# A two-block transformer on one core: the context norm placed inside the second feed-forward stage, its key products placed among the norms that follow

## The chip, the cores and the metric

The kernel runs on one core of one Trainium2 chip. The metric is the device time of one execution in microseconds (us), and the median of the runs shown is compared. Everything is float32.

## The reference, cut to what matters

A first block (256 tokens, width 1024) ends in a feed-forward layer, `y = conv_ffn(rms_norm(x))`, `x = x + rms_norm(y)`. The second block then takes `x` and a separate context of 256 tokens. Both are normed and modulated with their own shift and scale, and both go through the same input projections:

```
u  = modulate(rmsnorm(x,   norm1_g), sh1,  sc1)
uc = modulate(rmsnorm(ctx, norm1_g), sh1c, sc1c)
pl = split_proj(u,  w_in)      # queries, keys, values, gates, ...
pc = split_proj(uc, w_in)      # of the context, keys, values and gates alone are used
```

After that come a chunked recurrence (mLSTM) and a differential attention over context and latent keys, their merge, and a mixture of 32 experts (384 slabs of weights of 1 MB). The context and its norm depend on nothing in the first block. `x` depends on all of it.

## The kernel before

The activations lie transposed: 128 features in the partitions, 8 tiles of 256 tokens. The weights come in slabs of 1 MB. SP loads them in the order of a table, `SCHEDULE` (L59), into a ring of five slots, and waits before each load until the slab five places earlier has been used (`slab_used`, L388). TensorE multiplies in units: one unit (`product`) is 16 matmuls of 128x256, of which the trace records two each, so 32 records. The units go round three PSUM banks, and a unit waits until the unit three before it has been read.

The order on each engine is written out by hand, and the engines meet by semaphores. Around the change it is this:

- **Second feed-forward, in** (`ffn_in(1)`, TensorE L746): 22 units, one slab each. Per unit VectorE scales the bank (L1388) and adds two taps of a convolution (L1399), ScalarE makes the first tap (L1090) and a Silu (L1096), and VectorE multiplies (L1408). Unit 0 comes with the norm n7, whose squares VectorE adds up first (`presum`, L1380), so that one matmul (`presummed`, L623) gives the mean.
- **Second feed-forward, out** (`ffn_out(1, "n8")`, L638 and L649), with the squares of its result (L1078) and the mean for the norm n8 (`stat`, L607) at its end.
- **The norms n8, nc and n9.** A norm is a chain over three engines: squares on ScalarE (L1051), the mean by 8 matmuls with a constant matrix (`stat`, L607), a square root on ScalarE (`root`, L1059), a reciprocal on VectorE (`rstd`, L1352), and the scaled tiles. n8 norms the feed-forward's result and adds it to `X` (`residual`, L1368 and L1371). nc is the context's: SP loads it into `CT` (L477) once the feed-forward has ended, and VectorE and ScalarE write its modulated form `UC` (L1547, L1188). n9 norms `X`, and its modulated form is `H` (the same lines).
- **The first projections of the second block**: `mq` (2 slabs, 2 units, from `H` alone), the gates (64 matmul records of 16 columns, L767), `mk` (2 slabs, 4 units: each slab times `UC` and times `H`), then `cumf` (L777), `mv` and the rest.

TensorE's order there reads:

```
ffn_out(1, "n8")
stat("nc", 1, mean)
pe.wait_ge(sem("nc_root"), before("nc_root") + 1)
stat("n9", 0, mean)
stage("mq", H, "n9_h", busy=7)     # 7 matmuls without use ahead of the wait
...                                # gates
two("mk")
pe.wait_ge(sem("logf"), 1)         # then cumf
```

The last 40% of the time are the experts, whose slabs go round 16 slots (`first_load` L464, then L529).

Of the kernel before, what the change touches and what calls it, by code (L numbers as in the profile page):

```python
# [20 lines left out]
T = 256  # L21
D = 1024
KT = D // P
D_FF = 2816
FT = D_FF // P
TAPS = 31
GROUPS = 3
HEADS = 8
# [7 lines left out]
ADA_SLABS = 24  # L36
# [150 lines left out]
def build(nc, d_x, d_ctx, d_par, d_con, d_mmask, d_rows, d_gatew, d_routerw, d_b1, d_b2, d_cond, d_dense, d_experts, d_out):  # L187
    ctx = ExitStack()
    with ctx:
# [4 lines left out]
        norms = ["n0", "ln", "n1", "n2", "n3", "n4", "n6", "n7", "n8", "nc", "n9"]  # L194
        shared = {}
        for kind, count, stages in (
                ("sq", KT, norms + ["hm", "do", "n10", "n11"]), ("sum", 1, norms + ["n10", "n11"]),
                ("root", 1, norms + ["n10", "n11"]), ("x", KT, ["n1", "n3", "n6", "n8"]),
                ("h", KT, ["n0", "n2", "n4", "n5", "n7", "n11"]), ("h", KT, ["ln", "nc", "n9", "n10"]),
                ("p", KT, ["nc", "n9", "n10"]), ("tap", 2 * FT, ["ffn0", "ffn1"]), ("silu", FT, ["ffn0", "ffn1"]),  # L200
                ("act", FT, ["ffn0", "ffn1"]), ("cv", 2 * FT, ["ffn0", "ffn1"]), ("presum", KT - 1, ["n2", "n4", "n7"]),
                ("acc", KT, ["ffn0", "ffn1"]), ("out_slab", FT // 2, ["ffn0", "ffn1"])):
            for i, s in enumerate(stages):
                shared[f"{s}_{kind}"] = (f"{kind}_from_{stages[0]}_on", i * count)
# [71 lines left out]
        UC = tiles(area(NB, 2048), KT)  # L276
# [3 lines left out]
        HM = tiles(area(NB + 9216, 2048), KT)  # L280
# [144 lines left out]
        for i in range(2):  # L425
            second.append((FIRST_UNIT["mq"] + i, [MQ[:, 2 * i + j, :] for j in range(2)]))
        for name, to in (("mk", MK), ("mv", MV), ("dq", DQ), ("dk", DK), ("dv", DV)):
            for i in range(SLABS_OF[name]):
                if name == "dq":
                    second.append((FIRST_UNIT[name] + i, [to[:, 2 * i + j, :] for j in range(2)]))  # L430
                    continue
                for half in range(2):
                    if name in ("mk", "dk"):
# [23 lines left out]
        def _(sp):  # L457
# [8 lines left out]
            for g in range(DENSE_SLABS):  # L466
# [72 lines left out]
        def _(pe):  # L539
# [80 lines left out]
            def presummed(name):  # L620

                pe.wait_ge(sem(name + "_presum"), before(name + "_presum") + KT - 1)
                nc.tensor.matmul(banks[STAT][:, T:2 * T], mean, SQ[:, 0, :], start=True, stop=True)\  # L623
                    .then_inc(sem(name + "_sum"), 1)
# [145 lines left out]
            two("mk")  # L770
# [274 lines left out]
        def _(act):  # L1045
            def square(name, src, ready=None, sq=SQ):

                for c in range(KT):
# [31 lines left out]
            def ffn_in(layer):  # L1080
                name = f"ffn{layer}_in"
                for j in range(FT + 1):
                    if j < FT:
# [96 lines left out]
            ffn_in(1)  # L1180
            squared_acc(1, "n8")
            root("n8", 0)

            def shifted(name, v, m, dst):

                for c in range(KT):
# [22 lines left out]
            take(0, 2)  # L1209
# [5 lines left out]
            take(2, len(second))  # L1215
# [128 lines left out]
        def _(dve):  # L1344
# [29 lines left out]
            def presum(name):  # L1374

                for c in range(1, KT):
# [5 lines left out]
            def ffn_in(layer):  # L1382
                name = f"ffn{layer}_in"
                for j in range(FT + 1):
                    if j < FT:
# [145 lines left out]
            ffn_in(1)  # L1531

            dve.wait_ge(sem("ada_done"), ada_products(ADA_SLABS))
            for v in range(2):
                me(V.tensor_tensor(MOD[:, 0:16, v], MOD[:, 0:16, v], par[:, PAR["ada_b"]:PAR["ada_b"] + 16], ALU.add))
                me(V.scalar_tensor_tensor(GS1[:, :, v], MOD[:, 8:16, v], 1.0, par[:, PAR["norm1"]:PAR["norm1"] + 8],
                                          ALU.add, ALU.mult))
            dve.wait_ge(sem("rows_in"), 16)
            lam = rows[:, 0:256].rearrange("p (a b d) -> p a b d", a=2, b=2)
            me(V.tensor_tensor(tiles(LW, 2), lam[:, :, 0, :], lam[:, :, 1, :], ALU.mult))  # L1540
            V.tensor_reduce(LAM[:, 0:2], tiles(LW, 2), AX.X, ALU.add).then_inc(sem("lam_dot"), 1)
            residual("n8", rstd("n8", 0), acc, lambda c: ("ffn_post", 8 + c))

            def modulated(name, r, src, gain, dst):

                for c in range(KT):
# [11 lines left out]
            modulated("nc", rstd("nc", 1), CT, lambda c: GS1[:, c, 1:2], UC)  # L1558
# [4 lines left out]
            take(0, 2)  # L1563
# [15 lines left out]
            take(2, 6)  # L1579
# [347 lines left out]
```

## Time and profile before

| | |
|---|---|
| time, median of 3 runs | 2514.79 us (2513.84 to 2515.28) |
| time of the profiled execution | 2513.32 us |
| its span, first to last instruction | 2511.2 us |
| mean granted clock of TensorE | 0.989 of full speed |
| TensorE busy | 2391.6 us (95%) |
| VectorE busy | 760.0 us (30%) |
| ScalarE busy | 412.0 us (16%) |
| moved by DMA | 606.98 MB, mean 242 GB/s |

The span is 2.1 us shorter than the time of the same execution. The busy shares are averages over stages with different limits. So the stretches around the change are read one by one: which engine waits there, for what, and how long each step takes.

### The profile page before, as it was taken

The page shows a single profiled execution, that of the slowest core. Times are in us where ns is not written, and L with a number is a line of the kernel's source. Part 1 is how long each engine was busy: PE and PEld are TensorE (multiplying, and loading weights), DVE is VectorE, ACT ScalarE, POOL GpSimd, SP SyncE. Part 2 cuts the span into 40 slices and gives each one's busy share as a digit, 9 for nine tenths or more (in the row PEclk, how much of TensorE's full clock was granted, in tenths as well). Part 3 has the DMA queues.
Part 4 walks back from the last instruction along what each step waited for, and adds up shares of the span by engine and source line. Part 5 has one row for each costly group of instructions (what it writes and reads, how often), then busy time and mean ns, then how long its engine had stood idle before and what let it go on. Part 6 is the DMA issues. An engine that isn't in the chain of part 4 may idle for free.

```text
span 2511.2 us, 32943 instructions
## 1 busy us (share of the span) xinstructions
PE 2391.6 (95%) x13498; PEld 1800.1 (72%) x13498; DVE 760.0 (30%) x1846; ACT 412.0 (16%) x941; POOL 0.2 (0%) x4
## 2 busy tenths in 40 slices
PE   8899999999899999999988898999999999999998
PEld 7688888888788887988866586555555555555554
DVE  5833374210434312000244642222212111111212
ACT  4232202010232203000023422110101010101101
POOL 0000000000000000000000000000000000000000
PEclk9999999999999999899999999999999999999999
DMA  6034475664224442132122173999999999999996
GB/s 254 34 118 151 151 285 218 219 235 172 78 80 147 156 155 110 58 117 84 67 84 84 51 289 128 395 421 421 421 422 421 422 421 422 421 421 421 422 422 271
DMA packets 84281, 606.98 MB, mean 242 GB/s; under 512 B 9376, under 2 KB 9760, under 8 KB 10560
## 3 DMA queue, kind: packets, MB, share of 16 engines
q1 hardware_dynamic: 84192, 605.73, 61.1%
q8 instruction: 63, 1.03, 0.2%
q14 instruction: 26, 0.21, 0.0%
HBM read 604.65 MB, written 1.05 MB: 241 GB/s over the span
## 4 chain that ended last, share of the span: by engine, by line
PE 72%; SPq 15%; DVE 6%; ACT 3%; issue 2%; DMA 2%; DVEq 0%; ACTq 0%
PE bank L567 27%; SPq L529 15%; PE bank L980 10%; PE bank L564 8%; PE bank L638 5%; PE bank L1007 5%; PE bank L556 3%; DVE arena L1478 2%; PE bank L581 2%; PE bank L943 2%; PE bank L974 2%; PE bank L607 1%; DMA arena<-in_experts 1%; PE bank L718 1%; PE bank L649 1%
## 5 line engine op out<-in xcount | busy, mean ns | idle before, releaser
L567 PE MATMUL bank<-arena,ring 128*128 128x256 f32 x3296 | 716.3, 380 | 0.0
L567 PEld LDWEIGHTS bank<-arena,ring 128*128 128x128 f32 x3296 | 629.0, 191 | 83.9
L980 PE MATMUL bank<-arena 128*64 128x256 f32 x2048 | 293.7, 383 | 6.8 <-DMA arena<-in_experts 4.4
L980 PEld LDWEIGHTS bank<-arena 128*64 128x64 f32 x2048 | 173.7, 137 | 96.8 <-issue 20.0
L1839 DVE TENSOR_SCALAR arena<-bank 128x256 f32<-128x256 f32 x64 | 27.2, 425 | 698.2 <-PE bank L980 698.2
L564 PE MATMUL bank<-ring,arena 128*128 128x256 f32 x896 | 196.3, 382 | 0.0
L564 PEld LDWEIGHTS bank<-ring,arena 128*128 128x128 f32 x896 | 171.8, 192 | 23.2
L980 PE MATMUL bank<-ring,arena 128*64 128x256 f32 x1280 | 176.3, 382 | 8.0 <-DMA ring<-in_experts 5.1
L980 PEld LDWEIGHTS bank<-ring,arena 128*64 128x64 f32 x1280 | 104.6, 137 | 75.7 <-issue 13.9
L1007 PE MATMUL bank<-arena 128*64 128x512 f32 x512 | 140.1, 594 | 3.0 <-ACT arena L1326 3.0
L638 PE MATMUL bank<-arena,ring 128*128 128x256 f32 x576 | 124.6, 380 | 0.0
L638 PEld LDWEIGHTS bank<-arena,ring 128*128 128x128 f32 x576 | 109.7, 190 | 14.6
L980 PE MATMUL bank<-spare,arena 128*64 128x256 f32 x768 | 117.5, 383 | 0.2
L1311 ACT ACTIVATE arena<-arena 128x256 f32<-128x256 f32 x64 | 26.7, 417 | 456.3 <-DVE arena L1839 456.2
L1007 PEld LDWEIGHTS bank<-arena 128*64 128x64 f32 x512 | 49.8, 137 | 66.3 <-issue 66.3
L1456 DVE SCALAR_TENSOR_TENSOR arena<-ring,arena 128x1024 f32<-128x1024 f32 x64 | 74.9, 1220 | 73.6 <-DMA ring<-in_dense 73.6
L1399 DVE SCALAR_TENSOR_TENSOR arena<-arena,par 128x254 f32<-128x254 f32 (+1 forms) x176 | 73.3, 479 | 51.0 <-ACT arena L1090 51.0
L581 PE MATMUL bank<-arena,ring 128*128 128x256 f32 x384 | 87.0, 384 | 0.0
L1090 ACT ACTIVATE arena<-arena,par 128x256 f32<-128x256 f32 x88 | 48.0, 592 | 229.8 <-DVE arena L1388 229.8
L980 PEld LDWEIGHTS bank<-spare,arena 128*64 128x64 f32 x768 | 69.2, 137 | 22.7 <-issue 5.0
L581 PEld LDWEIGHTS bank<-arena,ring 128*128 128x128 f32 x384 | 72.2, 191 | 18.1 <-issue 9.1
L974 PE MATMUL bank<-arena 32*64 32x256 f32 x512 | 83.1, 400 | 0.9 <-ACT arena L1306 0.9
(263 smaller groups left out, 2159.2 us busy)
## 6 DMA issues: line engine op xcount, KB each, us to landing
arena<-in_experts SPq DMA_DIRECT2D x192, 1024.0 KB, 25.9
ring<-in_dense SPq DMA_DIRECT2D x186, 1024.0 KB, 4.8
ring<-in_experts SPq DMA_DIRECT2D x120, 1024.0 KB, 26.5
spare<-in_experts SPq DMA_DIRECT2D x72, 1024.0 KB, 25.9
con<-in_con SPq DMA_DIRECT2D x1, 1248.0 KB, 12.3
X<-in_x SPq DMA_DIRECT2D x1, 1024.0 KB, 5.0
arena<-in_cond SPq DMA_DIRECT2D x1, 1024.0 KB, 17.7
arena<-in_ctx SPq DMA_DIRECT2D x1, 1024.0 KB, 4.7
```

The costliest lines, as they stand in the source:

```text
L529: sp.dma_start(expert_slab(j), src).then_inc(slot_sem(j), 16)
L556: ins = nc.tensor.matmul(half_of(u, j), w[:, k, j * P:(j + 1) * P], src[:, k, :], start=(k == 0 and j == 0), stop=(k == KT - 1), skip_grou ...
L564: ins = nc.tensor.matmul(o, src[:, k, j * P:(j + 1) * P], w[:, k, :], start=(k == 0), stop=(k == KT - 1))
L567: ins = nc.tensor.matmul(o, w[:, k, j * P:(j + 1) * P], src[:, k, :], start=(k == 0), stop=(k == KT - 1))
L581: ins = nc.tensor.matmul(o, w[:, k, j * P:(j + 1) * P], H[:, k, :], start=(k == 0), stop=(k == KT - 1))
L638: ins = nc.tensor.matmul(banks[WORK + m // 2][:, (m % 2) * T:(m % 2 + 1) * T], w[:, kk, m * P:(m + 1) * P], F_ACT[:, k, :], start=(k == 0 ...
L943: ins = nc.tensor.matmul(banks[4 + b][:, (c % 4) * P:(c % 4 + 1) * P], U2T[:, t, c * P:(c + 1) * P], SEL[:, t, :], start=(t == 0), stop=(t ...
L974: nc.tensor.matmul(o, ONEH[:, e * CAP:(e + 1) * CAP], B1[:, i * T:(i + 1) * T], start=True, stop=False)
L980: ins = nc.tensor.matmul(o, XGT[:, k, e * CAP:(e + 1) * CAP], w[:, k, :], start=False, stop=(k == KT - 1))
L1007: ins = nc.tensor.matmul(banks[2 + half][e * CAP:(e + 1) * CAP, :], ACTT[:, k, e * CAP:(e + 1) * CAP], w[:, kk, half * 512:(half + 1) * 51 ...
L1399: ins = V.scalar_tensor_tensor(o, F_U[j % 2][:, half, 0:T - back], par_col("ffn_dw", (layer * 3 + 2 - back) * 44 + c), o, ALU.mult, ALU.add)
L1456: V.scalar_tensor_tensor(JUNK[:, n % 3, :], w[:, j, :], 1.0, CSR[:, v, :], ALU.mult, ALU.mult, accum_out=MOD[:, 2 * i + j, v:v + 1]).then_ ...
```

## The change

1. The context is loaded right before slab 1 of `ffn1_in`, after the attention's last head has been written (`att_out`), and no more behind the whole feed-forward.
2. The norm nc runs inside `ffn_in(1)`, by a function that ScalarE and VectorE call at the head of each unit j: the squares at j = 3 to 6, their sum on VectorE at j = 5 to 8, one matmul with the sum after unit 10 on TensorE, the root at j = 12, the reciprocal at j = 14, scaling at 15 to 18 and shift at 16 to 19, two tiles each. The work that makes the modulation (six small VectorE instructions) moves from the feed-forward's end to j = 2.
3. In `SCHEDULE`, `mk` stands ahead of `mq`. TensorE's order after the feed-forward is: unit mk0 x `UC`, the mean for n9, mk1 x `UC`, mk0 x `H`, mk1 x `H`, the gates, then both `mq` units. A slab of `mk` is given back when its `H` unit has ended. The seven matmuls without use are gone.
4. `UC` lies where `HM` lies later, as the old place is in use by the feed-forward.

```diff
-    ("mq", 2, 2), ("mk", 2, 4), ("mv", 4, 8),
+    ("mk", 2, 4), ("mq", 2, 2), ("mv", 4, 8),
...
-        UC = tiles(area(NB, 2048), KT)
...
-        HM = tiles(area(NB + 9216, 2048), KT)
+        UC = HM = tiles(area(NB + 9216, 2048), KT)
...
+            elif name == "mk":
+                unit_ready(eng, FIRST_UNIT[name] + 2 + i)
...
-                if g == SLAB_AT["mq", 1]:
-
-                    sp.wait_ge(sem("ffn1_out_slab"), before("ffn1_out_slab") + 11)
+                if g == SLAB_AT["ffn1_in", 1]:
+
+                    sp.wait_ge(sem("att_out"), HEADS)
                     sp.dma_start(CT, d_ctx).then_inc(sem("ctx_in"), 16)
...
-            stage("ffn1_in", H, first=1, count=21)
+            stage("ffn1_in", H, first=1, count=10)
+            presummed("nc", 0)
+            stage("ffn1_in", H, first=11, count=11)
             ffn_out(1, "n8")
-            stat("nc", 1, mean)
-            pe.wait_ge(sem("nc_root"), before("nc_root") + 1)
-            stat("n9", 0, mean)
...
-            stage("mq", H, "n9_h", busy=7)
-
             pe.wait_ge(sem("nc_h"), before("nc_h") + KT)
+            product(FIRST_UNIT["mk"], SLAB_AT["mk", 0], UC)
+            stat("n9", 0, mean)
+            product(FIRST_UNIT["mk"] + 1, SLAB_AT["mk", 1], UC)
+            product(FIRST_UNIT["mk"] + 2, SLAB_AT["mk", 0], H,
+                    wait_chunk=lambda k: pe.wait_ge(sem("n9_h"), before("n9_h") + k + 1))
+            product(FIRST_UNIT["mk"] + 3, SLAB_AT["mk", 1], H)
...
-            two("mk")
+            stage("mq", H)
...
+            def context_norm(j):
+
+                if j == 3:
+                    act.wait_ge(sem("ctx_in"), 16)
+                    act.wait_ge(sem("n7_sum"), before("n7_sum") + 1)
+                if 3 <= j < 7:
+                    square("nc", lambda c: CT[:, c, :], first=2 * j - 6, end=2 * j - 4)
+                if j == 12:
+                    root("nc", 0)
+                if 16 <= j < 20:
+                    shifted("nc", 1, 0, UC, first=2 * j - 32, end=2 * j - 30)
...
+            ffn_in(1, context_norm)
+            squared_acc(1, "n8")
+            root("n8", 0)
...
-            act.wait_ge(sem("ctx_in"), 16)
-            square("nc", lambda c: CT[:, c, :])
-            root("nc", 1)
             square("n9", lambda c: X[:, c, :], "n8_x")
             root("n9", 0)
-            shifted("nc", 1, 0, UC)
             shifted("n9", 0, 0, H)
...
-            take(0, 2)
+            take(0, 4)
...
+            def context_norm(j):
+
+                if j == 2:
+                    first_shift()
+                if 5 <= j < 9:
+                    presum("nc", max(2 * j - 10, 1), 2 * j - 8)
+                if j == 14:
+                    rstd("nc", 0)
+                if 15 <= j < 19:
+                    modulated("nc", RS[:, 0:T], CT, lambda c: GS1[:, c, 1:2], UC, first=2 * j - 30, end=2 * j - 28)
...
+            ffn_in(1, context_norm)
+            residual("n8", rstd("n8", 0), acc, lambda c: ("ffn_post", 8 + c))
...
-            modulated("nc", rstd("nc", 1), CT, lambda c: GS1[:, c, 1:2], UC)
             modulated("n9", rstd("n9", 0), X, lambda c: GS1[:, c, 0:1], H)
```

**TensorE, from the end of the second feed-forward to the first instruction of cumf.** Before, without what only repeats (L649 is the feed-forward's last product; L607 the means of n8, nc and n9, in this order 4, 8 and 8 of the 20; L543 the matmuls without use; L556 and L567 units; L767 the gates; L777 cumf):

```order
L649 MATMUL bank<-arena,ring 128x256 x8
L607 MATMUL bank<-arena,con 128x256 [waits sq_from_n0_on] x12
L607 MATMUL bank<-arena,con 128x256 [waits sq_from_n0_on,root_from_n0_on]
L607 MATMUL bank<-arena,con 128x256 [waits sq_from_n0_on] x7
L543 MATMUL bank<-con 128x256 [waits read0,slab2]
L556 MATMUL bank<-arena,ring 128x256 [waits h_from_ln_on]
L567 MATMUL bank<-arena,ring 128x256 [waits read1,slab3]
L767 MATMUL bank<-small,arena 128x16 [waits gatew_in,x_from_n1_on,h_from_ln_on]
L567 MATMUL bank<-arena,ring 128x256 [waits read2,slab4,h_from_ln_on]
L777 MATMUL bank<-arena,con 128x4 [waits logf]
```

Of the change (its lines stand 2 to 5 lower: L651, L609, L569, L558, L772, L782):

```order
L651 MATMUL bank<-arena,ring 128x256 x8
L609 MATMUL bank<-arena,con 128x256 [waits sq_from_n0_on] x4
L569 MATMUL bank<-arena,ring 128x256 [waits read0,slab2,h_from_ln_on]
L609 MATMUL bank<-arena,con 128x256 [waits sq_from_n0_on] x8
L569 MATMUL bank<-arena,ring 128x256 [waits read1,slab3]
L558 MATMUL bank<-arena,ring 128x256 [waits h_from_ln_on,read2,slab2]
L569 MATMUL bank<-arena,ring 128x256 [waits read0,slab3]
L772 MATMUL bank<-small,arena 128x16 [waits gatew_in,x_from_n1_on]
L569 MATMUL bank<-arena,ring 128x256 [waits read1,slab4]
L782 MATMUL bank<-arena,con 128x4 [waits logf]
```

The eight matmuls of nc's mean are gone from here, n9's eight stand between two units with `UC`, and between the gates and cumf there are two units where there were four.

**ScalarE, inside the second `ffn_in`, at j = 12.** Of the change (L1097 is the first tap, L1103 the Silu, L1062 and L1064 the root):

```order
L1097 ACTIVATE arena<-arena,par 128x256 x2
L1103 ACTIVATE arena<-arena 128x256
L1062 ACT_TABLE_LOAD
L1062 ACTIVATE small<-small 128x1
L1064 ACTIVATE arena<-bank,small 128x256
L1097 ACTIVATE arena<-arena,par 128x256 x2
L1103 ACT_TABLE_LOAD
L1103 ACTIVATE arena<-arena 128x256
```

Before, the pair of L1090 and L1096 (now L1097 and L1103) repeats there with nothing between; the root's three instructions and two loads of a function table are new in this place.

## Rows read from the trace of the kernel before

**Rows 1.** The page, part 4: the chain that ended last, by engine.
```profile
PE 72%; SPq 15%; DVE 6%; ACT 3%; issue 2%; DMA 2%; DVEq 0%; ACTq 0%
```

**Rows 2.** Windows, expert stage: busy of PE, PEld, DVE, ACT, POOL, PEclk, DMA share, GB/s.
```profile
1520.00:1560.00 40.00, 32.41 (x154) 25.85 (x153) 15.80 (x66) 13.18 (x27) 0.00 (x0) 0.87 0.28 105
...
1700.00:1800.00 100.00, 98.60 (x722) 55.76 (x720) 18.70 (x60) 11.01 (x21) 0.00 (x0) 1.00 1.01 421
```

**Rows 3.** Waits of SP's queue: us in total, times, longest us.
```profile
SPq L464 <- PE bank L980: 71.8, 12, 30.3
```

**Rows 4.** Timeline of PE, the mean of n8: start us, us, line, operation.
```profile
973.70 1.89 PE L607 MATMUL bank<-arena,con 128*128 128x256 f32 x8
```

**Rows 5.** The chain in order of time, n8 to cumf: start us, us, what.
```profile
973.89 4.74 DMA arena<-in_ctx
...
979.13 6.48 PE bank L607 x16
...
986.55 3.71 PE bank L607 x16
...
994.39 7.17 PE bank L556 x32
...
1008.47 10.12 PE bank L767 x64
1018.59 29.60 PE bank L567 x128
```

**Rows 6.** Groups by line from 751 to 897 us: busy us, mean ns, idle.
```profile
L567 PE MATMUL bank<-arena,ring 128*128 128x256 f32 x672 | 145.2, 380 | 0.0
```

**Rows 7.** Timeline of DVE, end of n8 and the norm n9.
```profile
983.41 0.75 DVE L1371 TENSOR_TENSOR X<-X,arena 128x256 f32<-128x256 f32 x2
...
991.10 1.75 DVE L1352 RECIPROCAL arena<-arena 128x256 f32<-128x256 f32 x1
992.88 3.26 DVE L1547 SCALAR_TENSOR_TENSOR arena<-X,small,arena 128x256 f32<-128x256 f32 x8
```

**Rows 8.** Timeline of ACT, the norm n9 (and nc's eight shifts ahead of its own).
```profile
986.00 2.55 ACT L1051 ACTIVATE arena<-X 128x256 f32<-128x256 f32 x8
...
990.28 0.47 ACT L1059 ACTIVATE arena<-bank,small 128x256 f32<-128x256 f32 x1 [1.64 <-PE bank L607]
990.66 6.47 ACT L1188 ACTIVATE arena<-arena,small 128x256 f32<-128x256 f32 x16
```

**Rows 9.** Windows around the norms and the gates, columns as in rows 2.
```profile
979.00:986.00 7.00, 6.47 (x16) 4.93 (x16) 5.16 (x15) 2.68 (x10) 0.00 (x0) 0.59 1.02 428
...
1008.00:1013.00 5.00, 5.00 (x42) 4.95 (x40) 0.76 (x2) 0.00 (x0) 0.00 (x0) 0.90 0.63 210
1013.00:1018.00 5.00, 5.00 (x25) 5.00 (x25) 0.00 (x0) 0.00 (x0) 0.00 (x0) 0.50 0.00 0
```

**Rows 10.** Timeline of DVE, last step of the chain that gives logf.
```profile
1021.20 0.39 DVE L1576 SCALAR_TENSOR_TENSOR arena<-arena 128x16 f32<-128x16 f32 x2 [1.93 <-ACT arena L1214]
```

**Rows 11.** Timeline of DVE: a presum, and first and last instruction now at j = 2.
```profile
746.78 3.59 DVE L1380 TENSOR_TENSOR arena<-arena 128x256 f32<-128x256 f32 x7
...
900.61 0.17 DVE L1535 TENSOR_TENSOR small<-small,par 128x16 f32<-128x16 f32 x1
...
901.75 0.29 DVE L1541 TENSOR_REDUCE small<-small 128x2 f32<-128x128 f32 x1
```

**Rows 12.** Timeline of DVE, start of a unit of the second ffn_in.
```profile
771.95 0.69 DVE L1388 TENSOR_TENSOR arena<-bank,arena 128x512 f32<-128x512 f32 x1 [3.05 <-PE bank L567]
```

**Rows 13.** Timeline of ACT, a table load and a unit of the same stage.
```profile
759.97 1.28 ACT L1096 ACT_TABLE_LOAD   x1
...
772.68 1.09 ACT L1090 ACTIVATE arena<-arena,par 128x256 f32<-128x256 f32 x2 [5.51 <-DVE arena L1388]
```

**Rows 14.** Timeline of SP: after the attention, and in the feed-forward's second half.
```profile
713.48 44.91 SPq L501 DMA_DIRECT2D ring<-in_dense  x6
...
930.73 14.14 SPq L501 DMA_DIRECT2D ring<-in_dense  x3
```

More of the change, by code:

```diff
@@ L190, in build @@
         sems = {}
[L194 removed]
+        norms = ["n0", "ln", "n1", "n2", "n3", "n4", "n6", "n7", "nc", "n8", "n9"]
         shared = {}
@@ L424, in build @@
         second = []
-        for i in range(2):
-            second.append((FIRST_UNIT["mq"] + i, [MQ[:, 2 * i + j, :] for j in range(2)]))
-        for name, to in (("mk", MK), ("mv", MV), ("dq", DQ), ("dk", DK), ("dv", DV)):
+        for half in range(2):
+            for i in range(2):
+                second.append((FIRST_UNIT["mk"] + 2 * half + i, [MK[:, 2 * i + j, half * T:(half + 1) * T] for j in range(2)]))
+        for name, to in (("mq", MQ), ("mv", MV), ("dq", DQ), ("dk", DK), ("dv", DV)):
             for i in range(SLABS_OF[name]):
-                if name == "dq":
+                if name in ("mq", "dq"):
                     second.append((FIRST_UNIT[name] + i, [to[:, 2 * i + j, :] for j in range(2)]))
@@ L618, in out_stage, with presummed @@
                 stat(stat_name, 0, mean, first=6)
-            def presummed(name):
+            def presummed(name, half=1):
                 pe.wait_ge(sem(name + "_presum"), before(name + "_presum") + KT - 1)
-                nc.tensor.matmul(banks[STAT][:, T:2 * T], mean, SQ[:, 0, :], start=True, stop=True)\
+                nc.tensor.matmul(banks[STAT][:, half * T:(half + 1) * T], mean, SQ[:, 0, :], start=True, stop=True)\
                     .then_inc(sem(name + "_sum"), 1)
@@ L1045, in _, with square @@
         def _(act):
-            def square(name, src, ready=None, sq=SQ):
-                for c in range(KT):
+            def square(name, src, ready=None, sq=SQ, first=0, end=KT):
+                for c in range(first, end):
                     if ready:
@@ L1078, in squared_acc, with ffn_in @@
                         nc.scalar.activation(SQ[:, i, :], acc(i), ACT.Square).then_inc(sem(name + "_sq"), 1)
-            def ffn_in(layer):
+            def ffn_in(layer, beside=None):
                 name = f"ffn{layer}_in"
                 for j in range(FT + 1):
+                    if beside:
+                        beside(j)
                     if j < FT:
@@ L1179, in _, with shifted @@
             root("n7", 1)
[L1180 to L1186, printed above, removed]
+            def context_norm(j):
[8 more added lines that the diff above has]
+                    shifted("nc", 1, 0, UC, first=2 * j - 32, end=2 * j - 30)
+            def shifted(name, v, m, dst, first=0, end=KT):
+                for c in range(first, end):
                     act.wait_ge(sem(name + "_p"), before(name + "_p") + c + 1)
@@ L1214, in _ @@
             nc.scalar.activation(AB, AB, ACT.Ln, bias=ONE_COL).then_inc(sem("f_ln"), 1)
-            take(2, len(second))
+            take(4, len(second))
             def raw_gate(n):
@@ L1372, in residual, with presum @@
                          .then_inc(sem(name + "_x"), 1)
-            def presum(name):
-                for c in range(1, KT):
+            def presum(name, first=1, end=KT):
+                for c in range(first, end):
                     dve.wait_ge(sem(name + "_sq"), before(name + "_sq") + c + 1)
@@ L1380, in presum, with ffn_in @@
                     V.tensor_tensor(SQ[:, 0, :], SQ[:, 0, :], SQ[:, c, :], ALU.add).then_inc(sem(name + "_presum"), 1)
-            def ffn_in(layer):
+            def ffn_in(layer, beside=None):
                 name = f"ffn{layer}_in"
                 for j in range(FT + 1):
+                    if beside:
+                        beside(j)
                     if j < FT:
@@ L1530, in _ @@
             rstd("n7", 1)
[L1531 to L1546, printed above, removed]
+            def first_shift():
+                dve.wait_ge(sem("ada_done"), ada_products(ADA_SLABS))
+                for v in range(2):
+                    me(V.tensor_tensor(MOD[:, 0:16, v], MOD[:, 0:16, v], par[:, PAR["ada_b"]:PAR["ada_b"] + 16], ALU.add))
+                    me(V.scalar_tensor_tensor(GS1[:, :, v], MOD[:, 8:16, v], 1.0, par[:, PAR["norm1"]:PAR["norm1"] + 8],
+                                              ALU.add, ALU.mult))
+                dve.wait_ge(sem("rows_in"), 16)
+                lam = rows[:, 0:256].rearrange("p (a b d) -> p a b d", a=2, b=2)
+                me(V.tensor_tensor(tiles(LW, 2), lam[:, :, 0, :], lam[:, :, 1, :], ALU.mult))
+                V.tensor_reduce(LAM[:, 0:2], tiles(LW, 2), AX.X, ALU.add).then_inc(sem("lam_dot"), 1)
@@ new lines, in context_norm, with modulated @@
+            def context_norm(j):
[7 more added lines that the diff above has]
+                    modulated("nc", RS[:, 0:T], CT, lambda c: GS1[:, c, 1:2], UC, first=2 * j - 30, end=2 * j - 28)
+            def modulated(name, r, src, gain, dst, first=0, end=KT):
+                for c in range(first, end):
@@ L1562, in _ @@
             me(V.tensor_scalar(LAM[:, 5:6], LAM[:, 4:5], -1.0, -LAM_INIT, ALU.mult, ALU.add))
-            take(0, 2)
+            take(0, 4)
             dve.wait_ge(sem("gates"), 1)
@@ L1578, in _ @@
                 me(ins) if d == 0 else ins.then_inc(sem("logf"), 1)
-            take(2, 6)
+            take(4, 6)
             dve.wait_ge(sem("cumf"), 1)
```

4 lines of the change are left out of this document (2 added, 2 removed).

## The prediction

> **What bounds the kernel now.** First the chain that ended last, by engine [rows 1]: 72% of it is TensorE, 15% SP's queue. The queue's part lies in the last 500 us, where the experts' slabs come at 421 GB/s with a DMA share of 1.01 [rows 2]. So the question is whether time won early reaches the end. Between 1520 and 1560 us the DMA share is 0.28, and the queue's first loads of experts wait for TensorE, 71.8 us in 12 waits [rows 3]. The stream starts when TensorE lets it, so a start earlier by x us ends it earlier by x.
>
> Then the stretch itself, from the chain in order of time. The eight records of n8's mean end at 973.70 + 1.89 = 975.6 us [rows 4]. TensorE waits for the context, whose load of 4.74 us was issued only at 973.89 [rows 5]. It does the 16 records of nc's mean (6.48 us) and the 16 of n9's (3.71 us), waits again, and starts `mq` at 994.39 [rows 5]. The first unit whose result is used begins 18.8 us after 975.6. Then come 14.08 us of `mq`, 10.12 us of gates and 29.60 us of `mk`, up to 1048.19 [rows 5]. The stretch is **72.6 us** from 975.6 to cumf.
>
> **The change, part by part.** A unit is 32 records. The 672 records of the feed-forward, 21 units, took 145.2 us without a pause [rows 6], so a unit is 6.91 us and 16 records are 3.45 us.
>
> *TensorE after the feed-forward.* The two units with `UC` need nothing of the first block, and `UC` is ready long before.
> - mk0 x `UC`: 975.6 to 982.5 us.
> - The mean for n9, 3.45 us: to 986.0. Can it run without a pause? The last tile of `X` is written at 983.41 + 0.75 = 984.16 [rows 7], and its square takes 0.4 us (8 squares in 2.55, overlapping) [rows 8], so it is there at 984.6. The matmul that needs it starts at 985.5. No pause.
> - mk1 x `UC`: to 992.9. Beside it the chain of n9 runs: root 0.47 [rows 8], reciprocal 1.75, first scaled tile 0.5 [rows 7], first shift 0.5 (16 in 6.47) [rows 8]. The first tile of `H` is there at 986.0 + 3.3 = 989.3, the last at 992.1 (8 scalings in 3.26 and one shift). TensorE wants the first at 992.9. No pause, with 3.6 us to spare.
> - mk0 x `H` and mk1 x `H`: 13.8 us, to 1006.7.
> - The gates 10.12 us, as before, to 1016.8.
> - The two `mq` units: 13.8 us at the full clock, and a surcharge. Before, the 128 records behind the gates took 29.60 us where four units are 27.65, so 1.95 us were lost at their start. I take the same 1.95. To 1032.6.
>
> *In `ffn_in`* TensorE gets one more matmul, two records, 0.43 us.
>
> The sum is 6.91 + 3.45 + 6.91 + 13.82 + 10.12 + 13.82 + 1.95 + 0.43 = **57.4 us**, against 72.6: **15.2 us less**. Removed are 3.5 us of waiting for the context, nc's mean (6.48) and most of the wait for n9, and two units of 6.91 fill what is left.
>
> *What bounds the surcharge and the gates.* The granted clock was 0.90 from 1008 to 1013 us and 0.50 from 1013 to 1018, that is, it fell from 2.4 to 1.2 GHz while TensorE did gates of 16 columns; 42 records went in the first window and 25 in the second [rows 9]. If it did not fall, 64 gate records would take 64 x 5/42 = 7.6 us and nothing would be lost behind them: 2.5 + 1.95 = 4.5 us less than my sum. If it fell at their start, 64 x 5/25 = 12.8 us, 2.7 more, and a stretch like that of 979 to 986, where 16 records took 6.47 us at 0.59 [rows 9] instead of 3.45, would add 3.0. I take the value in between, the one measured on the same 64 matmuls. What precedes the gates differs: before, TensorE paused twice in the 33 us ahead of them, now it doesn't, so a fall would come later rather than earlier. The Trainium skill ("TensorE: Matmul & The Clock Gate", Part 1) says that the clock is either half or full, never between, and that the number of slow matmuls differs from run to run of one and the same kernel. By it neither end of this bound can be excluded, and the sum would be 57.4 with some 5 us to either side. The trace agrees as far as it goes: 0.50 in one window, 1.00 in most.
>
> *The cover of the gate arithmetic.* cumf waits for logf, which was ready at 1021.20 + 0.39 = 1021.6, 3.0 us after the gates' end at 1018.6 [rows 5, 10]. It was covered by 29.6 us of `mk`, now by 15.8 us of `mq`. Nothing to pay. If it were late, cumf would be next.
>
> *The work put inside `ffn_in`.* VectorE gets six small instructions at j = 2 (900.61 to 902.04, 1.4 us), a presum (3.6 us) [rows 11], a reciprocal (1.75) and eight scalings (3.3) [rows 7]: 10.0 us. It waits 3.05 us of each 6.91 us unit for TensorE [rows 12]. The largest piece at one j is 1.75. ScalarE gets eight squares (2.6), eight shifts (3.2), and at j = 12 a root (0.47) with two table loads of 1.28 [rows 13], 3.0 us: 8.8 us in all. It waits 5.51 us of each unit [rows 13]. Both fit unit by unit; at j = 12 the later Silu holds up VectorE's product by about 3.0 us, which just uses up its 3.05 idle. TensorE wants a bank back only two further units later, 13.8 us. The cost is nothing. Without that cover it would be 18.8 us (rival D). Nor do the stage's last units carry anything new.
>
> *Loads.* Slab 1 of `ffn1_in` was issued at 713.48 [rows 14], behind o's first unit. The context now goes ahead of it, once the attention's last head is out, and takes 4.74 us. The slab is wanted at about 751, where the row of the 672 records begins [rows 6], so some 30 us are free. `mk` stands where `mq` stood: the three loads from 930.73 to 944.87 [rows 14] end with the first slab after the feed-forward's, so mk0 is issued by 945, 30 us before its use, and mk1 some 7 us later. The two slabs of `mk` are held until 999.8 and 1006.7; the loads behind them are mv1 and mv2, wanted after 1050. Nothing.
>
> **The number.** The profiled execution took 2513.32 us, 2.1 above its span. Less 15.2 that is 2498.1. The median shown is 1.5 us above that execution, so for the median I predict 2514.79 - 15.2 = **2499.6 us**.
>
> **Rivals.** A measurement of this kernel can tell about 0.2%, 5 us, from no change.
> - **A, the forecast**: chance 0.84, 2495 to 2505 with the clock's two bounds (+5.7, -4.5).
> - **B, n9 comes late.** TensorE works in order, and n9's mean now stands behind a unit: it ends at 986.0, 1.4 us after the last square. If the chain to the first tile of `H` took over 6.9 us instead of 3.3, TensorE would wait at mk0 x `H`, and the clock could fall as at 979 us: 2 us of waiting and 3.0 of slowness make 2504.6. For it: TensorE's 7 matmuls without use are gone, so a wait would be idle. Against: 3.6 us of room. Chance 0.06.
> - **C, nothing reaches the end.** If the experts' stream, 421 GB/s for 900 us, were already held by DMA when it starts, the time would stay 2514.8. For it: SP's 15% of the chain. Against: the share of 0.28 at its start [rows 2] and the waits of the first loads [rows 3]. Chance 0.05.
> - **D, slower: the three banks run dry in `ffn_in`.** If VectorE's lag adds up beyond the 13.8 us of two units, TensorE stands still inside the feed-forward, in front of each further piece. It decides from about 3 us of added work per unit on, kept up for several units. In full series the added work is 18.8 us, and a clock that falls at its three stops (squares, root, shifts, 3.0 each as at 979) makes it 27.8: 27.8 - 15.2 = 12.6 us slower, 2527.4. For it: the two table loads and three engines in turn for one norm. Against: each piece is smaller than the idle time of its unit. Chance 0.05. The Trainium skill ("ScalarE: Activation LUTs", What ACT_TABLE_LOAD costs, and its advice to do all of one table set before switching) puts each switch at about 2.66 us with a drain. By it j = 12 would hold 2 x 2.66 + 0.47 = 5.8 us in 5.51 of idle, 0.3 us over, once. The trace shows 1.28 us and the next instruction right behind.
>
> **How the numbers follow.** The likeliest case gives 2499.6. The range 2495.0 to 2505.0 holds A with both ends of the clock and B. C and D lie outside, 0.10 together, and some of A's ends. Faster by over 5 us: A and B, 0.90. Within 5 us: C, 0.05. Slower: D, 0.05.
>
> **What would show it.** In the changed profile the records of mk0 x `UC` begin within 0.1 us of the end of n8's mean, and TensorE has no idle time until cumf; that stretch is about 57 us. `ffn_in`'s units keep 6.91 us each with one break of 0.43. SP issues the context at about 707 us, one unit before 713.48. The first expert load comes 15 us earlier, and DMA runs at 421 GB/s as long as before. I am wrong if TensorE waits at mk0 x `H` (B), if the start of the stream moves and the end doesn't (C), or if the 22 units of `ffn_in` take over 153 us (D). A different clock around the gates would show as a size error alone.

## The result, and the profile after

| | before | after |
|---|---|---|
| median of the runs timed together | 2514.32 us (2512.52 to 2515.28, 4 runs) | **2540.03 us** (2538.78 to 2541.35, 4 runs) |
| ratio after to before | | **1.0096**, 95% interval 1.0084 to 1.0108 |
| profiled execution, its span | 2513.32 us, 2511.2 us | 2540.68 us, 2538.8 us |

The changed kernel is 25.7 us slower. The prediction was 15.2 us faster, with 0.05 for slower. It was wrong, and not by a size: the sign is the other one.

The part of the program that was changed did what was forecast. This is the chain that ended last in the changed kernel, in order of time from n8's mean to cumf (start us, us, what):

```profile
975.48 1.73 PE bank L609 x8
977.21 6.91 PE bank L569 x32
984.11 3.45 PE bank L609 x16
987.57 6.91 PE bank L569 x32
994.47 6.91 PE bank L558 x32
1001.38 6.91 PE bank L569 x32
1008.29 8.43 PE bank L772 x64
1016.72 15.85 PE bank L569 x64
1032.57 4.36 PE bank L782 x40
```

Each row starts where the row above ends. From n8's end at 977.21 to cumf at 1032.57 are 55.4 us, where it was 72.6 [rows 4, 5]. cumf starts 15.6 us earlier than the 1048.19 of before, as n8's mean itself ends 1.6 us later here. That lead lasts: the first matmul of the loop over the pairs of experts starts at 1544.59 instead of 1560.09 us, 15.5 earlier.

The loss lies behind that point. Three places of the page show it; its header, the queue that brings TensorE's instructions (packets, MB, share of 16 engines) and the chain by engine, after:

```profile
span 2538.8 us, 32902 instructions
...
q8 instruction: 126, 2.06, 0.3%
...
PE 87%; DVE 7%; ACT 3%; issue 3%; DMA 0%; ACTq 0%; DVEq 0%
```

and the same of before:

```profile
span 2511.2 us, 32943 instructions
...
q8 instruction: 63, 1.03, 0.2%
```

SP's queue had 15% of the chain [rows 1] and has none now; TensorE has 87%. The bound has changed. And the queue that brings instructions moved twice as many packets of 16 KB in an execution of 41 instructions fewer.

The chain in the expert loop, after (start us, us, what), tells when. L1012 is the down projection that ends a pair, L979 and L985 are the first matmuls of the next:

```profile
1645.22 13.95 PE bank L1012 x64
1659.17 2.26 issue
1661.43 0.75 PE bank L979 x4
1662.18 2.26 PE bank L985 x9
1664.44 2.33 issue
1666.77 5.38 PE bank L985 x23
...
1711.39 13.95 PE bank L1012 x64
1725.34 0.58 PE bank L979 x4
...
1768.59 13.95 PE bank L1012 x64
1782.54 2.02 issue
```

The loop's body holds two pairs. Within it, at 1725.34, the next pair follows at once. Where TensorE jumps back, at 1659.17 and at 1782.54, it stands still twice, 2.26 us and, after 13 matmuls, 2.33 us, and waits for nothing that the profile shows. The matmuls between and behind the pauses are slow. The windows there (columns as in rows 2) give the clock:

```profile
1659.17:1672.15 12.98, 8.39 (x39) 5.11 (x39) 0.00 (x0) 1.07 (x2) 0.00 (x0) 0.62 1.01 418
1700.00:1800.00 100.00, 94.19 (x648) 53.30 (x642) 16.00 (x53) 8.90 (x18) 0.00 (x0) 0.95 1.00 411
```

The granted clock fell, to 0.62 over these 13 us; in a stretch without a jump it is 1.00 [rows 2]. The waits of TensorE (line, us in total, times, longest) say how often, after:

```profile
PE bank L985 <- issue: 17.8, 7, 3.6
PE bank L979 <- issue: 14.7, 7, 2.3
```

There are 7 of each, one for each jump back. One repetition takes 1768.59 - 1645.22 = 123.4 us; before it took 1775.13 - 1660.72 = 114.4 us (the starts of the same L1007 rows in its chain). That is 9.0 us more, 4.6 of it pauses and 4.4 slow matmuls; seven times that would be 63 us.

The whole loop, from its first matmul record to the end of its last, took 932.4 us before (1560.09 to 2492.44) and takes 975.9 now (1544.59 to 2520.50): 43.5 us more. Less the lead of 15.5 these are 28.0 us, and the two spans differ by 27.6. The jumps cost more than the 43.5, because before the change TensorE waited in the loop for the experts' stream: its wait list has these rows (line, us in total, times, longest), and the changed kernel's has none of them.

```profile
PE bank L980 <- DMA arena<-in_experts: 7.3, 10, 0.7
PE bank L980 <- DMA ring<-in_experts: 5.1, 7, 0.7
PE bank L980 <- DMA spare<-in_experts: 2.2, 3, 0.7
```

Together these are 14.6 us. TensorE is now the later of the two. Runs below, without the stream, put the price of the seven jumps at **60.4 us** and that former wait at 16.9.

### The profile page after: what moved, and what is told of

It reads as the page before. It is cut to its first block, busy times and chain, and to the rows that moved or that the text cites. A ratio compares the mean times of both kernels' runs of the same rounds, so it can differ in the third digit from the quotient of the medians.

```text
span 2538.8 us, 32902 instructions
## 1 busy us (share of the span) xinstructions
PE 2407.8 (95%) x13470; PEld 1807.1 (71%) x13470; DVE 762.2 (30%) x1853; ACT 415.4 (16%) x943; POOL 0.2 (0%) x4
## 3 DMA queue, kind: packets, MB, share of 16 engines
HBM read 604.65 MB, written 1.05 MB: 239 GB/s over the span
## 4 chain that ended last, share of the span: by engine, by line
PE 87%; DVE 7%; ACT 3%; issue 3%; DMA 0%; ACTq 0%; DVEq 0%
PE bank L569 26%; PE bank L985 19%; PE bank L1012 9%; PE bank L566 8%; PE bank L640 5%; PE bank L979 3%; PE bank L948 3%; PE bank L558 2%; DVE arena L1495 2%; PE bank L583 2%; PE bank L959 1%; PE bank L609 1%; PE bank L720 1%; PE bank L651 1%; ACT arena L1266 1%
## 5 line engine op out<-in xcount | busy, mean ns | idle before, releaser
L569 PE MATMUL bank<-arena,ring 128*128 128x256 f32 x3296 | 716.9, 380 | 0.0
L569 PEld LDWEIGHTS bank<-arena,ring 128*128 128x128 f32 x3296 | 627.5, 190 | 85.5
L985 PE MATMUL bank<-arena 128*64 128x256 f32 x2048 | 318.9, 407 | 17.8 <-issue 17.8
L985 PEld LDWEIGHTS bank<-arena 128*64 128x64 f32 x2048 | 190.4, 145 | 115.3 <-issue 51.3
L985 PE MATMUL bank<-ring,arena 128*64 128x256 f32 x1280 | 176.2, 382 | 0.0
L985 PEld LDWEIGHTS bank<-ring,arena 128*64 128x64 f32 x1280 | 104.4, 137 | 67.0 <-issue 18.5
L1012 PE MATMUL bank<-arena 128*64 128x512 f32 x512 | 140.1, 593 | 3.1 <-ACT arena L1341 3.1
L985 PE MATMUL bank<-spare,arena 128*64 128x256 f32 x768 | 117.5, 382 | 0.0
L979 PE MATMUL bank<-arena 32*64 32x256 f32 x512 | 85.2, 405 | 15.6 <-issue 14.7
L1326 ACT ACTIVATE arena<-arena 128x256 f32<-128x256 f32 x64 | 26.7, 417 | 442.2 <-DVE arena L1868 442.1
L1012 PEld LDWEIGHTS bank<-arena 128*64 128x64 f32 x512 | 49.8, 137 | 66.3 <-issue 66.3
L985 PEld LDWEIGHTS bank<-spare,arena 128*64 128x64 f32 x768 | 69.1, 137 | 22.3 <-issue 6.2
L1097 ACT ACTIVATE arena<-arena,par 128x256 f32<-128x256 f32 x88 | 48.0, 592 | 221.3 <-DVE arena L1405 221.3
## 6 DMA issues: line engine op xcount, KB each, us to landing
arena<-in_cond SPq DMA_DIRECT2D x1, 1024.0 KB, 17.8
```

What stands on the lines that cost most here:

```text
L569: ins = nc.tensor.matmul(o, w[:, k, j * P:(j + 1) * P], src[:, k, :], start=(k == 0), stop=(k == KT - 1))
L979: nc.tensor.matmul(o, ONEH[:, e * CAP:(e + 1) * CAP], B1[:, i * T:(i + 1) * T], start=True, stop=False)
L985: ins = nc.tensor.matmul(o, XGT[:, k, e * CAP:(e + 1) * CAP], w[:, k, :], start=False, stop=(k == KT - 1))
L1012: ins = nc.tensor.matmul(banks[2 + half][e * CAP:(e + 1) * CAP, :], ACTT[:, k, e * CAP:(e + 1) * CAP], w[:, kk, half * 512:(half + 1) * 51 ...
```

## The experiments

**The question.** The changed program has fewer instructions for TensorE ahead of the loop. Counted in the compiled program, there are 57 fewer: 14 matmuls of two records each and their weight loads, and a wait. The loop's two pairs are 1,690 instructions in both kernels (both counts stand in no profile; the runs below test them at the borders that follow from them). A packet of 16 KB holds 256 instructions. The pause after 13 matmuls puts a border between two such blocks there; so the loop begins at place 227 of a block in the changed kernel and reaches into 8 blocks (227 + 1,690 = 1,917, over 7 x 256 = 1,792). 57 instructions more and it begins at place 28 and reaches into 7 (1,718), as before. The 63 additional packets are 7 x 9.

- The theory: a loop over 8 blocks is fetched anew at each jump back, one over 7 isn't. What counts is its place.
- A first rival: the moved work itself slows the expert loop, since the stream starts earlier and the queues meet otherwise.
- A second rival: the form or the length of the compiled program, or chance, and not the place.

The edit for all "pad" runs is the same and computes nothing: increments of a semaphore that nobody waits for, in TensorE's program where it is idle for 10.7 us at about 80 us, waiting for `glu`. N is in the label.

```diff
+            for _ in range(N):
+                pe.sem_inc(sem("pad"), 1)
             for c in (6, 7):
                 pe.wait_ge(sem("glu"), c + 1)
```

**The changed kernel with 57 increments.**

> The changed kernel with 57 semaphore increments more in TensorE's program, placed where TensorE waits some 10 us in the first convolution; nothing else. Theory F (instruction fetch): the change made TensorE's program 57 instructions shorter ahead of the expert loop, so that the loop of 1,690 instructions now touches 8 blocks of 256 instructions (16 KB, the size of an instruction packet) instead of 7, and is fetched anew in each of its 7 repetitions. 57 instructions put it back where it stood before. F expects 63 instruction packets of 16 KB instead of 126, no pause of TensorE behind the jump, and 2514.3 - 15.6 = about 2498.7 us. Theory S (stream): the experts' transfers start 15.6 us earlier and run against TensorE in another phase. S expects what the changed kernel has: about 2540 us, and the pauses stay.

Measured: 2502.89 us (2502.33 to 2503.43) against 2515.28, ratio **0.9946** (0.9932 to 0.9959). The same change, with 57 instructions that do nothing, is faster than before, and 37 us faster than without them. Its page:

```profile
q8 instruction: 63, 1.03, 0.2%
...
PE 72%; SPq 16%; DVE 6%; ACT 3%; issue 2%; DMA 2%; DVEq 0%; ACTq 0%
```

63 packets, the stream back in the chain, no pause in the loop. The first rival falls: the moved work and the earlier stream are all still there. The loop starts at 1549.40, 10.7 us earlier than before, and the span is 10.2 us shorter. The median gained 12.4 us and not 15.2. In the profiled run the clock was lower at the gates and behind them, as the chain shows (start us, us, what; 8.43, 15.85 and 4.36 in the changed kernel):

```profile
1005.41 10.81 PE bank L774 x64
1016.22 16.76 PE bank L569 x64
1032.98 5.90 PE bank L784 x40
```

**The kernel before with 199 increments**, which put its loop at place 28 + 199 = 227.

> The kernel before with 199 = 256 - 57 semaphore increments more in the same place, so that its expert loop lies in the blocks as in the changed kernel. F expects 126 instruction packets, 9 us more per repetition of the loop, that is 7 x 9 = 63 us on TensorE, of which the wait for the experts' transfers before covered some 20: about 2514.3 + 41 = 2555 us. S expects about 2514, since nothing of the stream is changed.

Measured: 2572.03 us (2569.34 to 2575.39), ratio 1.0222 (1.0205 to 1.0238), with 127 packets. The waits of TensorE:

```profile
PE bank L720 <- issue: 26.7, 1, 26.7
PE bank L982 <- issue: 15.8, 7, 3.4
PE bank L976 <- issue: 14.5, 7, 2.2
```

The loss appears in a kernel that has nothing of the change: its loop takes 975.6 us, where the changed kernel's takes 975.9. The increments were not free, as L720's row says: the convolution starts at 99.45 instead of 82.62 us, 16.8 later. Less that, 2555.2 us remain, 40 above before; the loop itself is 43.2 longer. Between them these two runs make place the cause, and not the change.

**Only the context's norm moved.** The order `mq`, gates, `mk` is as before; 57 increments keep the loop in 7 blocks (place 56).

```diff
-    ("mk", 2, 4), ("mq", 2, 2), ("mv", 4, 8),
+    ("mq", 2, 2), ("mk", 2, 4), ("mv", 4, 8),
...
+            stat("n9", 0, mean)
+            stage("mq", H, "n9_h", busy=7)
+
             pe.wait_ge(sem("nc_h"), before("nc_h") + KT)
-            product(FIRST_UNIT["mk"], SLAB_AT["mk", 0], UC)
-            stat("n9", 0, mean)
...
-            stage("mq", H)
+            two("mk")
```

> The norm of the context alone moved into the second feed-forward; the order of the products is that of the kernel before (both mq units with H behind the norm n9, then the gates, then mk), and 57 increments keep the expert loop in 7 blocks. From the prediction's sum: the mean for n9 ends at the last square, about 985, and mq begins at about 988.5 instead of 994.4, less 0.4 for the added matmul: about 5.5 us less than before, 2509. The other 9 to 10 us of the change would then be those of the two units with UC that fill the wait. If the mere move of the context's norm gave all of it, the time would be 2499.

Measured: 2506.18 us (2505.99 to 2507.76), ratio 0.9963 (0.9950 to 0.9976), 9.1 us faster. Its chain:

```profile
978.87 6.40 PE bank L606 x16
...
988.66 7.17 PE bank L555 x32
...
1002.74 8.39 PE bank L768 x64
...
1040.84 4.36 PE bank L778 x40
```

n9's mean and its chain stay bare, as was expected: `mq` starts at 988.66 (988.5 was expected), 14.2 us after n8's end at 974.5, where it was 18.8. So the moved norm is worth 4.6 us in the chain. Another 1.7 us are gates at a higher clock; the rest of the 9.1 lies ahead of n8's end (1.1 us in the profiled executions) and in the scatter of the kernel before. From n8's end to cumf there are 66.3 us here and 55.4 in the changed kernel, with gates of 8.39 and 8.43: the two key units in the chain are worth the other 10.9 us. By the medians of the two timed kernels with 57 increments they gain only 3.3 us (2506.18 against 2502.89), as the gates, the units behind them and cumf ran slower in the second.

**Four other places.** They look for the border, and test whether 57 was luck.

> The changed kernel with 24 increments. By theory F the first instruction of the loop stands at place 227 of a block of 256 in the changed kernel (TensorE pauses there after 13 matmuls of the loop); with 24 more at 251: still 8 blocks, about 2540 us, 126 packets, and the second pause comes within the first two matmuls of the loop. A theory in which any shift would do, or one in which the 57 merely delay something, expects the time to lie between 2498 and 2540.

> The changed kernel with 36 increments: place 7, 7 blocks. F expects a step, about 2498.7 us and 63 packets, where 24 increments still gave 2540.

> The changed kernel with 124 increments: place 95; the loop of 1,690 instructions just ends within its seventh block (1,785 of 1,792). F expects about 2498.7 us and 63 packets.

> The changed kernel with 140 increments: place 111; the loop runs over into an eighth block. F expects about 2540 us and 126 packets, with the second pause some 140 instructions, about 70 matmul records, behind the jump. If the number of instructions were not what counts, or if more of them only helped, it would stay at 2499.

| kernel | place | blocks | packets | us |
|---|---|---|---|---|
| changed + 36 | 7 | 7 | 63 | 2494.71 |
| before, and changed + 57 | 28 | 7 | 63 | 2514.32, 2502.89 |
| changed + 124 | 95 | 7 | 63 | 2508.43 |
| changed + 140 | 111 | 8 | 109 | 2518.49 |
| changed | 227 | 8 | 126 | 2540.03 |
| changed + 24 | 251 | 8 | 126 | 2551.25 |

(The four are one run each; before beside them: 2519.77 us, one run.) The packets are 63 in every row of 7 blocks and more in every row of 8, on both sides: between 95 and 111, where 1,690 more cross 1,792, and between 251 and 7, where the block border passes the loop's first instruction. Twelve increments more, 36 instead of 24, take 57 us off. With 124 and 140 they no longer fit the idle 10.7 us: the wait there is 15.0 and 17.6 us, so they cost 4.3 and 6.9 us by themselves; less that, 124 stands at 2504.1. At place 251 the loop's first five instructions are a block's end, and the second pause comes after two matmuls and is longer, nothing executing beside it:

```profile
1659.23 2.12 issue
1661.35 0.64 PE bank L981 x2
1661.98 4.60 issue
```

The run with 140 missed part of its expectation. It has 46 packets more, 5 x 9 + 1, and pauses in five of seven repetitions, one each:

```profile
PE bank L981 <- issue: 10.8, 5, 2.2
```

The second pause that was expected some 70 records later isn't there; the packet of the next block comes 5.7 us after the first one's (1668.81, 1674.54), and the first block's 145 instructions keep TensorE busy that long. Why two repetitions go without any fetch is open.

**When the packets come.** The trace has the start of each instruction packet. In the kernel before, the last one of the loop comes at 1658.01 us, 16.7 ahead of the first jump's matmul at 1674.67, and the next at 2491.05, at the loop's end. In the changed kernel nine come for one repetition: at 1781.63, just ahead of the pause that begins at 1782.54, then at 1787.50, 1793.84, 1808.09, 1825.64, 1840.95, 1861.50, 1878.46 and 1895.53. This fits a store of eight blocks, filled in order, in which the next block is fetched when one is entered. Over 7 blocks, the eighth fetch takes the last free place and nothing is lost. Over 8, the fetch of a ninth displaces the first, and from the jump on each block displaces the one that is needed next: eight for the loop and one beyond. At place 111 the loop ends nine instructions into its eighth block; at five of the seven jumps a packet comes 2.4 to 2.9 us ahead of the eight others (1666.11 before 1668.81), at the last two none comes. The store itself was not tested further.

**36 increments again, timed, and a control: before with 24 (place 52 by the count above, which the expectation puts at 50; 7 blocks either way).**

> The changed kernel with 36 increments once more, now timed in five rounds against the kernel before. The single look gave 2494.7 us beside 2519.8 of the kernel before. F expects faster by 15.2 us plus or minus the clock's falls (the version with 57 increments, also in 7 blocks, came out 12.4 us faster): between 2493 and 2503.

> A control: the kernel before with 24 increments, hidden in a wait of 10.7 us. Its loop begins at place 50 instead of 26, 7 blocks either way. F expects 63 packets and no difference beyond the scatter of the clock's falls, up to 5 us. If any shift of the program moved the time by tens of us, it would show here.

Measured: the first 2502.26 us (2494.84 to 2503.52, 6 runs) against 2515.72, ratio **0.9935** (0.9919 to 0.9951). The control 2516.88 us, ratio 0.9999 (0.9989 to 1.0009). So 24 increments that leave the loop in 7 blocks change nothing that can be measured, and the best version of all is the change with its loop moved. Its six runs lie on two levels, two at 2495 and four at 2501 to 2504. Two profiled executions of this program, at 2494.71 and 2501.22 us, show part of why. In the first the gates took 8.80 us (start us, us, what):

```profile
1005.22 8.80 PE bank L774 x64
```

In the second:

```profile
1006.88 10.52 PE bank L774 x64
```

The granted clock from 1015 to 1020 us was 0.80 in the first and 0.50 in the second. How long the clock stays down at the gates differs between executions of one and the same program. The gates make 1.7 of the 7.1 us by which the second enters the loop later; as much lies ahead of them, and 3.8 behind cumf.

**Why a repeated fetch is so dear.** Either the fetch waits behind the experts' bytes on busy DMA engines, or it takes its time in any case. The experts' loads are cut to an eighth, with and without the 57 increments.

```diff
-                    sp.dma_start(expert_slab(j), src).then_inc(slot_sem(j), 16)
+                    sp.dma_start(expert_slab(j)[:, 0:256], src[:, 0:256]).then_inc(slot_sem(j), 16)
```

> The changed kernel, whose expert loop loads only the first 256 of the 2,048 columns of each slab (the rest of a slab keeps the values of the first pass, so 7/8 of the experts' bytes from the third pair on are left out). The DMA engines are then mostly idle. Theory F1: a block of instructions that TensorE waits for stands behind the experts' bytes in the same DMA engines; then the two pauses of 2.3 us shrink to well under 1 us each, and TensorE's loop takes about 2 x 57.2 + 2 us. Theory F2: the pause is the fetch's own time; then it stays at 2.3 us each, and a repetition takes 123 us as now.

> The same with 57 increments, so that nothing is fetched again. TensorE alone sets the time of the loop: 2 x 57.2 = 114.4 us per repetition. Its difference to the kernel without the increments is what fetching costs without a stream beside it: by F1 a few us per repetition, by F2 9 us, 63 in all.

Measured, one run each: 2486.80 us with 126 packets, 2476.78 with 63. The chain of the first (start us, us, what) and its window of 1600 to 2400 us:

```profile
1657.63 0.65 PE bank L979 x4
1658.27 1.22 PE bank L985 x9
1659.50 1.05 issue
1660.55 2.81 PE bank L985 x23
```

```profile
1600.00:2400.00 800.00, 780.73 (x5700) 452.54 (x5700) 167.00 (x504) 82.64 (x161) 0.00 (x0) 1.00 0.24 71
```

With DMA at 0.24 instead of 1.01 the same 63 packets cost one pause, 1.05 us here and 1.2 at most, instead of two of 2.3, and the clock over these 800 us is 1.00. The loop takes 923.6 us in the first kernel and 915.5 in the second: 8.1 apart, 1.2 us for each jump. (The spans are 10.0 us apart; 1.9 of that lies ahead of the loop.) Beside the stream it is 975.9 - 915.5 = 60.4 us, **8.6 for each jump**. So the first holds: what makes a repeated fetch dear is the saturated stream beside it. Of the 60.4 us the wait list has 32.5 as pauses (17.8 + 14.7); the rest is matmuls at a lower clock behind them. What makes the clock fall was not isolated: after single pauses of 2.2 us, in the run with 140 increments, it was 0.94 from 1660 to 1690 us and 1.00 from 1780 to 1800.

The second of these kernels also gives TensorE's time alone in the loop: 915.5 us, 114.4 for each repetition. Before, with the stream, the first four repetitions took 114.4 to 114.5 us too, and the last three 119.4 to 119.6: the stream becomes the bound in the second half of the loop alone. In sum that was 932.4, 16.9 us of waiting. The account closes: **before, TensorE waited some 17 us for the stream; after, it never does, and 60 us of its own take their place.** 60.4 - 16.9 = 43.5, less the lead of 15.5 is 28.0, and the spans differ by 27.6.

**The same 57 increments behind the loop.** If the mere length of the program or another compiled form were at work (the second rival), this would help as well.

> The control for the place: the changed kernel with the same 57 increments behind the expert loop instead of ahead of it. F, in which only what lies ahead of the loop moves it over the block borders, expects the changed kernel's 2540 us and 126 packets, plus some us for the increments themselves, which nothing hides there (57 took under 10.7 us ahead of the first convolution). If the increments helped by anything but their place, it would come down towards 2503.

Measured in one run: 2556.88 us (before beside it 2516.05), 126 packets, and

```profile
PE bank L985 <- issue: 18.2, 7, 3.6
PE bank L979 <- issue: 14.7, 7, 2.2
```

The fourteen pauses stay. The increments themselves are not hidden there; the wait list has 9.2 us for them, behind the loop. The loop starts at 1552.06 instead of 1544.59, 7.5 us later, of which `mv` already has 3.9 (1040.86 instead of 1036.93) after slower gates and cumf; it takes 975.2 us, where it took 975.9; and behind it lie 9.4 us more. That is the whole difference of 16.2 us to 2540.68. Only instructions ahead of the loop help, and the second rival falls too.

## Why the prediction was wrong

- **TensorE after the feed-forward: right.** Predicted 57.0 us from n8's mean to cumf, besides 0.43 in `ffn_in`; measured 55.4. The plain units came out at 6.91, the means at 3.45. No pause before mk0 x `H`: B did not occur.
- **The gates and the surcharge: inside their bounds.** Predicted 10.12 and 13.8 + 1.95; measured 8.43 and 15.85 here, 10.81 and 16.76 with 57 increments. Together that is 24.3 and 27.6 us, where the sum had 25.9 and its ends 21.4 and 31.6.
- **The work inside `ffn_in`: right.** TensorE's records there take 379 ns each, where they took 380 [rows 6], with the one additional matmul. At j = 12 ScalarE still has 3.63 us of idle time ahead of its next tap, between the root's end and the second table load (start us, us, line, operation):

```profile
836.45 1.09 ACT L1097 ACTIVATE arena<-arena,par 128x256 f32<-128x256 f32 x2 [3.63 <-DVE arena L1405]
837.56 1.28 ACT L1103 ACT_TABLE_LOAD   x1
838.86 0.42 ACT L1103 ACTIVATE arena<-arena 128x256 f32<-128x256 f32 x1
```

  That speaks against D. The Trainium skill ("ScalarE: Activation LUTs", What ACT_TABLE_LOAD costs) adds a drain to the load at every switch; no drain shows here, as the load starts 0.02 us after the tap ends, and the Silu 0.02 us after its load of 1.28.
- **Loads: right.** The context is issued at 708.15 and the slab behind it at 714.66, and nobody waits for either.
- **"A start earlier by x us ends it earlier by x": this is the step that failed.** It came from [rows 1 to 3] and took two things for granted. One is that the stream stays the bound; it was, by 17 us, and that margin was never worked out, only the fact of SP's 15%. The other is that TensorE's time in the expert loop, code that the diff doesn't touch, can't change. TensorE's own time there grew by 60 us, 8.6 for each of seven jumps back, and the loop as a whole by 43.5. The sum counted 14 fewer matmuls as time saved and not as 57 instructions fewer ahead of a loop. With 57 or 36 put back the step holds: the loop starts 10.7 us earlier with 57 and the span is 10.2 shorter. The medians are 2502.89 and 2502.26 us, both within the range of 2495 to 2505, and the faster level (2494.7 to 2495.0) lies at its lower end. The forecast was for the kernel without them, though.
- **The rivals.** C and D ended at 2514.8 and 2527.4. Neither named anything behind the expert loop's start, so the 0.05 for slower was held by a mechanism that did not occur. The row that would have raised the question was on the page of before: 63 instruction packets for TensorE, a loop, and a change in the number of instructions ahead of it.

The rule for this stands in the Trainium skill ("Runtime: NRT & Kernel Launch", Instruction fetch mechanics): an engine's instructions come in blocks of 16 KiB or 256 instructions, into a memory that holds 2,048 of them for TensorE, and a taken branch to a block that isn't held forces a fetch before execution goes on. The runs agree with the block and the forced fetch. The section also speaks of two blocks, and by that every one of these loops would be fetched anew; those of 7 blocks never were (63 packets). By 2,048 instructions, eight blocks, a loop over 8 would just fit, and it was fetched anew (126 packets, and 109 at place 111). The same section says that the next page is fetched while the current one executes; with one of the eight places taken by that page, 7 blocks fit and 8 don't, and the nine packets for each jump and their times agree with it.

## What to carry to other kernels

Where an engine's program contains a loop near the size of what its instruction memory keeps, every edit ahead of the loop is also a change of the loop's place, and must be costed as such: count the instructions, count the blocks of 256 that the loop touches, and look at the number of instruction packets on the page before and after. If it grew, test with instructions that do nothing before judging the edit; here that turned a ratio of 1.0096 into 0.9935. And when a sum says that a lead reaches the end, work out by how much the present bound leads over the next one (here 17 us), since that margin is all that protects the sum.

## What the runs showed of the hardware

- A loop of 1,690 TensorE instructions brought no packets after its first pass when it touched 7 blocks of 256, and 9 packets for each jump back when it touched 8 (126 against 63 for 7 jumps). The times of the packets fit eight held blocks, one of them fetched ahead; that place 111 gave only 46 more isn't explained.
- Such a fetch cost 8.6 us a jump beside a stream of some 411 GB/s (4.6 of pauses, 4.0 of matmuls at a lower clock) and 1.2 us beside 71 GB/s.
- The 64 records of the gates took 8.15 to 11.13 us in the profiled runs, and one kernel's executions lay on two levels some 8 us apart. A difference of that size between two single runs of this kernel proves nothing.
- An increment of a semaphore by TensorE isn't free: 199 of them took 26.7 us by the row of L720, which is 0.13 us each. Up to 57 fitted into the wait of 10.7 us there.
